# Seventeen projection jobs of a hybrid encoder block, from feature form to token form

## The reference

```
h = x + 0.5 * norm(swiglu(norm(x)))                    # FFN 1, inner width 5632
proj = norm(h) @ w_in                                  # pooling | z | x,B,C | dt | gates
A:  p -> trailing means over 2, 4, 8, 16 tokens (4 groups of 512 channels) minus p
      -> 512x512 map per group -> scale -> @ w_pool_out
B:  x,B,C -> causal depthwise conv over 4 tokens + SiLU; chunked state-space scan in 8 groups
      (8 heads of 64 each); * SiLU(z); norm; @ w_ssd_out
h = h + norm((sigmoid(gA) * A + sigmoid(gB) * B) @ w_mix_out)
k, v = norm(mem) @ w_k, w_v;  q = norm(h) @ w_q        # 4 heads of 128, 256 memory tokens
h = h + norm(attention(q, k, v) @ w_xo)
h = h + 0.5 * norm(swiglu(norm(h)))                    # FFN 2
```

## Time and profile before

| | us |
|---|---|
| median of three runs | 2731.94 |
| the profiled execution's own time | 2732.21 |
| its span in the trace | 2730.5 |
| TensorE matmul busy | 2717.9 |
| VectorE busy | 1631.0 |
| ScalarE busy | 1289.9 |
| GpSimd busy | 345.9 |

### The profile page before, as it was taken

The page is one execution under the profiler, slowest core; times in us unless marked ns, Lnnn a source line. Parts: engine busy times, 40 slices in busy tenths (PEclk is TensorE's granted clock), DMA queues, the critical chain, the costliest instruction groups (busy, mean ns, idle before and its releaser), DMA issues.

```text
span 2730.5 us, 39496 instructions
## 1 busy us (share of the span) xinstructions
PE 2717.9 (100%) x14076; PEld 2336.3 (86%) x14076; DVE 1631.0 (60%) x1920; ACT 1289.9 (47%) x1442; POOL 345.9 (13%) x619
## 2 busy tenths in 40 slices
PE   9999999999999999999999999999999999999998
PEld 7888888888899889989999888888988888888887
DVE  5555555544577556787887775566565555554444
ACT  5444444444454544455554564445654444444443
POOL 1121212000000000002122201223002122120000
PEclk9999999999999999999999999999999999999999
DMA  7777767666666665567667676668567677776664
GB/s 234 205 210 201 209 200 207 200 197 196 173 186 195 201 200 182 170 184 213 183 190 216 179 210 202 203 228 227 162 180 210 194 212 207 202 208 199 197 197 161
DMA packets 286770, 541.48 MB, mean 198 GB/s; under 512 B 27504, under 2 KB 28400, under 8 KB 286416
## 3 DMA queue, kind: packets, MB, share of 16 engines
q1 hardware_dynamic: 263520, 504.00, 60.7%
q0 software_dynamic: 22976, 36.07, 5.0%
q10 hardware_dynamic: 176, 0.07, 0.0%
HBM read 519.53 MB, written 2.16 MB: 191 GB/s over the span
## 4 chain that ended last, share of the span: by engine, by line
PE 98%; DVE 1%; DMA 0%; ACT 0%; issue 0%; DVEq 0%; ACTq 0%
PE J L660 26%; PE J L662 26%; PE J L661 26%; PE J L694 5%; PE J L697 5%; PE J L696 5%; PE J L737 1%; PE A L962 1%; PE A L963 1%; PE A L961 1%; PE J L733 0%; PE J L709 0%; DMA raw<-in_w_mix_out_dram 0%; PE J L674 0%; PE J L676 0%; PE J L675 0%
## 5 line engine op out<-in xcount | busy, mean ns | idle before, releaser
L1509 DVE TENSOR_TENSOR wl<-raw,wh 128x1024 fp32r<-128x1024 f32 x950 | 1154.5, 1222 | 961.8 <-ACT wh L1093 956.2
L1093 ACT ACTIVATE wh<-raw 128x1024 fp32r<-128x1024 f32 x950 | 1005.1, 1060 | 1305.2 <-PE J L662 1046.5
L660 PE MATMUL J<-wh,ul 128*128 128x512 f32 x2016 | 786.0, 390 | 2.3 <-DVE wl L1509 2.1
L662 PE MATMUL J<-wl,uh 128*128 128x512 f32 x2016 | 784.5, 389 | 0.0
L661 PE MATMUL J<-wh,uh 128*128 128x512 f32 x2016 | 784.4, 389 | 0.0
L660 PEld LDWEIGHTS J<-wh,ul 128*128 128x128 f32 x2016 | 378.6, 188 | 82.1 <-issue 4.0
L662 PEld LDWEIGHTS J<-wl,uh 128*128 128x128 f32 x2016 | 378.5, 188 | 79.0
L661 PEld LDWEIGHTS J<-wh,uh 128*128 128x128 f32 x2016 | 378.6, 188 | 77.5
L694 PE MATMUL J<-ul,wh 128*128 128x256 f32 x1056 | 300.2, 284 | 0.0
L697 PE MATMUL J<-uh,wl 128*128 128x256 f32 x1056 | 298.8, 283 | 0.0
L696 PE MATMUL J<-uh,wh 128*128 128x256 f32 x1056 | 298.8, 283 | 0.0
(11 more groups left out here) (293 smaller groups left out, 2262.4 us busy)
## 6 DMA issues: line engine op xcount, KB each, us to landing
raw<-in_ffn_w_dram SPq DMA_DIRECT2D x528, 512.0 KB, 4.3
raw<-in_w_in_dram SPq DMA_DIRECT2D x257, 512.0 KB, 3.9
raw<-in_w_ssd_out_dram SPq DMA_DIRECT2D x64, 512.0 KB, 3.6
raw<-in_w_pool_out_dram SPq DMA_DIRECT2D x32, 512.0 KB, 4.1
raw<-in_w_mix_out_dram SPq DMA_DIRECT2D x32, 512.0 KB, 6.2
hraw<-turned POOLq DMA_DIRECT2D x320, 32.0 KB, 4.0
csb<-cs_dram POOLq DMA_DIRECT2D x16, 512.0 KB, 7.4
raw<-in_pool_w_dram SPq DMA_DIRECT2D x8, 512.0 KB, 4.7
```

Of the source, the lines that this page charges most:

```text
L660: nc.tensor.matmul(o[:, t], b, wh[:, r, kk], start=(k == 0 and kk == 0), stop=False)
L662: mm = nc.tensor.matmul(o[:, t], a, wl[:, r, kk], start=False, stop=(k == last_k and kk == CK - 1))
L1093: nc.scalar.activation(wh[:, r], raw[:, r], ACT.Copy).then_inc(high, 1)
L1509: nc.vector.tensor_tensor(wl[:, r], raw[:, r], wh[:, r].bitcast(F32), ALU.subtract).then_inc(low, 1)
```

## The change

All 17 jobs are issued in token form. For each of them there are now four steps where there was one: ScalarE copies the PSUM tile to SBUF with the row norm as its scale (`tokens_out`, two instructions; for k one plain copy), VectorE turns it by 32x32 squares (`turn_tokens`, two transposes), GpSimd issues 16 DMAs of 32 KB that carry the blocks to where pooling and convolution read (`move_tokens`), and the reader waits for all of them (`f_moved`). One buffer `f_turn` serves all jobs but k, and one number `f_turned` counts them.

The places move too. Pooling's window starts 4 chunks after the end of the job behind (`end(pw)+4`) instead of at the end of its own; the taps of C0 start 5 chunks after C0, those of B1 in C1 after the masked squares (5 chunks), those of C1 in the first x job (5 chunks), those of x 5 chunks after x. The SiLU of x, its eight transposes on TensorE and its copy move to the next group: transposes after 2 chunks of x, the scan after 5 (3 before). The subtractions of the decay rows are split around the variance. GpSimd loads the next `csb` rows first, then moves x, then y of the group before.

```diff
+            def move_tokens(name, dst):
+                pool.wait_ge(f_turned, f_number(name) + 1)
+                move_natural(dst, f_turn, f_moved)
...
+            for g in range(GROUPS):
+                if g < GROUPS - 1:
+                    pool.wait_ge(seg_ready, g + 1)
+                    load_csb(g + 1)
+                move_tokens(("x", g), x_in)
+                if g >= 1:
+                    move_y(g - 1)
...
+            def tokens_out(name, dst, i=None, per=0):
+                n = f_number(name)
+                act.wait_ge(used, lin(end(name), i, per))
+                if n >= 1 or i is not None:
+                    act.wait_ge(f_turned, lin(n, i, 1))
+                for t in range(T):
+                    a = nc.scalar.activation(dst[:, t], tok(slot(name))[:, t], ACT.Copy, scale=sr_u[:, t:t + 1])
+                a.then_inc(evacuated[slot(name)], 1)
...
-            def conv_in(name, i=None, per=0):
-                done(i, per)
-                o = bc_in if i is None and isinstance(name, str) else x_in
-                nc.vector.tensor_tensor(o[:], feat(slot(name)), rbc[:].unsqueeze(1).to_broadcast([P, M, S]),
-                                        ALU.mult).then_inc(evacuated[slot(name)], 1)
+            def turn_tokens(name, src, i=None):
                 dve.wait_ge(evacuated[slot(name)], lin(moved(name), i, 1))
+                turn_blocks(f_turn, src, f_turned)
             def conv_taps(name, dst, blk, i=None, per=0, blk_per=0):
...
+                dve.wait_ge(f_moved, lin(256 * (f_number(name) + 1), i, 256))
...
+            for g in range(3):
+                to(end(f"pin{g + 1}"))
+                turn_tokens(f"pin{g + 1}", f_raw)
+                if g == 0:
+                    dve.wait_ge(t_ready[1], use(1, "csT"))
+                    nc.vector.tensor_copy(cst[:], A[:, 1, 0, 0:P]).then_inc(t_moved[1], 1)
+                pool_mixed(g)
+                to(end(f"pw{g}") + 4)
+                pool_window(g + 1)
+                to(end(f"pw{g}") + 6 + g // 2)
+                pool_low(g + 1)
...
+                to(c0 + CD, i, per)
+                turn_tokens(("x", 0), zs, i)
+                if i is not None:
+                    to(c0 + CD + 1, i, per)
+                    finish_scale(0, i - 1)
+                to(c0 + CD + 4, i, per)
...
                 weigh(slice(0, HPG // 2), 0, i)
+                to(c0 + CD + 5, i, per)
+                if i is None:
+                    cb_masked(1, 1)
+                conv_taps(("x", 0), xc, 0, i, per, M)
```

More of the change, by code:

```diff
@@ L386, in hybrid_block, with f_number @@
         CONVS = ["B0", "C0", "B1", "C1", ("x", 0)]
+        TURNED_JOBS = ["pin0", "pin1", "pin2", "pin3", "B0", "C0", "B1", "C1"] + [("x", g) for g in range(GROUPS)]
+        def f_number(name):
+            return TURNED_JOBS.index(name)
         def turned_before(f):
@@ L591, in _ @@
             pool.wait_ge(cs_stored, 16)
+            for g in range(1, 4):
+                move_tokens(f"pin{g}", pool_x)
             pool.wait_ge(pooled_low, len(WINDOWS))
@@ L878, in _ @@
             claim("pin0")
-            after_halves("pin0", 1, feature=True)
-            feature_chunks("pin0", uh, ul, range(4, 7), CD - 1, before=pre_wait(1))
+            after_halves("pin0", 1)
+            token_chunks("pin0", uh, ul, range(4, 7), CD - 1, before=pre_wait(1))
             pe.wait_ge(normed, 2)
@@ L964, in ssd, with turn_x @@
                 mm.then_inc(t_ready[1], 1)
+            def turn_x(i=None):
+                pe.wait_ge(xc_silu, GROUPS if i is None else i)
+                n = use(0, ("xT", 0)) - 1
+                pe.wait_ge(t_moved[0], n + GROUPS - 1 if i is None else lin(n - 1, i, 1))
+                for t in range(T):
+                    for m in range(M):
+                        tr = nc.tensor.transpose(A[:, 0, t, m * P:(m + 1) * P], xc[:, m, t * P:(t + 1) * P], ident[:])
+                tr.then_inc(t_ready[0], 1)
             def group(i=None):
@@ L1265, in _ @@
             pre_norm_behind(1)
+            def tokens_out(name, dst, i=None, per=0):
[3 more added lines that the diff above has]
+                    act.wait_ge(f_turned, lin(n, i, 1))
+                for t in range(T):
+                    a = nc.scalar.activation(dst[:, t], tok(slot(name))[:, t], ACT.Copy, scale=sr_u[:, t:t + 1])
+                a.then_inc(evacuated[slot(name)], 1)
+            to(end("pin0"))
+            act.wait_ge(normed, 2)
+            tokens_out("pin0", f_raw)
             to(end("dt") + 2)
@@ new lines, in group @@
+                if i is not None:
+                    to(c0 + 1, i, per)
+                    weigh(slice(HPG // 2, HPG), 0, i - 1).then_inc(w_ready, 1)
+                    to(c0 + 3, i, per)
+                    scale_x(0, i - 1)
+                    to(c0 + 6, i, per)
+                    finish_gate(0, i - 1)
+                    to(c0 + 7, i, per)
+                else:
+                    to(c0 + 2)
+                dve.wait_ge(csb_loaded, lin(16 * T, i, 16 * T))
+                subtract(range(HPG // 2))
@@ L1992, in group @@
+                if i is not None:
                     finish_var(0, i - 1)
+                else:
+                    to(c0 + 3)
+                subtract(range(HPG // 2, HPG)).then_inc(seg_ready, 1)
                 if i is None:
                     to(c0 + 5)
[L1995 to L2001 removed]
@@ L2002, in group @@
-                for h in range(HPG):
-                    def scalar(row):
-                        return small[:, row, h:h + 1] if i is None else small[:, row, bass.ds(i * HPG + h, 1)]
-                    nc.vector.tensor_scalar(E[:, h, 0:P], csb[:, h, 0], scalar(CS), 0.0, ALU.subtract, ALU.min)
-                    nc.vector.tensor_scalar(E[:, h, P:2 * P], csb[:, h, 1], scalar(REM), 0.0, ALU.add, ALU.min)
-                    l = nc.vector.tensor_scalar(E[:, h, 2 * P:3 * P], csb[:, h, 1], scalar(CS + 1), 0.0, ALU.subtract, ALU.min)
-                    if h == HPG // 2 - 1:
-                        to(c0 + 7, i, per)
```

262 lines of the change are left out of this document (134 added, 128 removed).

## The result

| | before | after | ratio |
|---|---|---|---|
| time, median | 2732.07 us | 2746.65 us (2745.12 to 2748.52, 5 runs) | 1.0053, 95% interval 1.0040 to 1.0066 |
| profiled execution | 2732.2, span 2730.5 | 2745.12, span 2743.5 | |

The changed kernel is 14.6 us slower, where I had forecast 10 us faster. In the profiled executions the loss is 13.0 us of span, and this is what has to be explained: my sum ended at 2722.2 for the profiled one, so it misses 22.9.

A forecast was written before the change was run, and what follows sets the result against it. TensorE's instruction spacings bound the kernel. Savings of 21.8 and 0.5 us against waits of 6.2, 0.35, 3.3, 0.85 and 1.6 gave -10.0, from 2732.2 to 2722 us; range 2711 to 2734.

The forecast's parts named there:

- token form, with the first group's stall: All 17 jobs: 0.16 us less a chunk over 136 chunks, -21.8 us, and -0.5 for TensorE's waits in first z.
- groups 1 to 7, stops: TensorE waits 0.9 us for late splits at the end of z in each of seven groups: +6.2 us.
- B1, C1, first x and z: Waits in the first jobs' chain of turns and taps: 0.35, 3.3 and 0.85 us.
- pooling: TensorE waits for pooll 1.35 us in group 3 and 0.25 in group 1: +1.6 us.
- Rival D: Token form saves less, 4.2 us by the page's formula, if something else sets the spacing: 2740 us; chance 0.05.
- I take 4.1, the middle: Landing after the last of sixteen issues, before work needing the data starts: 4.1 us, from rows of 3.42 to 4.89.
- T = E + 18.0: Groups 1 to 7: the taps of x start 18.0 us after x's end, where no wait needs 17.1.
- at 5.5, the bound that I gave: Upper end for the landing, the median of mem_raw's moves: time 2740 us.
- each us later costs about 12: Each us of later landing costs about 12 us, as there are 12 waits.
- Rival B: Moves about 2 us slower, from y's scalings and transposes beside the issues and csb's 1 MB: 2746 us; chance 0.12.
- Rival C, the lock: VectorE's reciprocal and y scalings hold GpSimd's issue at most 1.0 us in seven groups: 2729 us; chance 0.16.
- C1's 3.3 us: C1's taps stand in the first x job, so z's first split is late and TensorE waits 3.3 us.

The follow-up runs named there:

- e5: The changed kernel without the moves of the eight x jobs; the taps of x read f_turn directly: 2717.45 us, 0.9945 of before.
- e2: The changed kernel with csb's load for the next group issued behind x's and y's moves instead of ahead of them: 2738.22 us, 1.0020 of before.
- e10: The changed kernel with csb's load issued behind the copy of X, taps at their old place: 2737.22 us, 1.0018 of before.
- e9: The changed kernel with x's taps one chunk later, csb's load behind the copy of X, the sums' store behind pin1's moves: 2719.02 us, 0.9951 of before.
- e7: The changed kernel with x's taps one chunk later and csb's load behind the moves of x and y: 2729.73 us, 0.9999 of before.
- e3: The changed kernel with x's moves first, then a wait for their landing, then csb's load and y's moves: 2745.40 us, 1.0049 of before.
- e11: The kernel of e9 once more, with more rounds beside the kernel before on one chip: 2718.37 us, 0.9949 of before.

## Why the prediction was wrong, point by point

| step | forecast, us | measured, us |
|---|---|---|
| token form, with the first group's stall | -22.3 | about -20 |
| groups 1 to 7, stops | +6.2 | +20.0 |
| the lower clock behind them | no term | +7 to +9, of a rest of 9.8 |
| B1, C1, first x and z | +4.5 | about 0 |
| pooling | +1.6 | +2.9 |

The second and third row are the 29.8 us by which seven periods exceed those of e5: 20.0 are the stops and 9.8 remain, of which six drops of 1.1 to 1.5 us are 7 to 9. With 0.4 for the squares of B and C the sum is +13, as measured; but the first row is itself a rest, so this sum is no proof of it.

- **Token form: right.** -1.24 instead of -1.28 a job. In e5 the waits over those of before make 5 us and the time is 14.9 below before, so the form brings about 20; the last 2 us are spread in pieces that I did not trace. Rival D is out.
- **The step that failed: "I take 4.1, the middle" for the landing, and with it T = E + 18.0.** The mechanism was right: late splits behind late taps stop TensorE at the start of each x job. Turn, issue and the formula for the stop were right within 0.3 us. The size of this term was not: the landing was 5.6 to 6.4 us, and the seven stops are 20.0 us instead of 6.2. I had noted that no row shows this way "beside a csb load just issued", and took a middle of rows without such a load. e2 and e10 bring it to 4.5 to 4.9 in eleven groups of fourteen by taking csb away; in the other three, and in the changed kernel's last group, it is 5.6 to 6.2 without csb, and why stays open. A case named as unlike the rows should have been priced at their upper end: at 5.5, the bound that I gave, the sum was 2740.
- **The step that was missing: what a stop does behind itself.** No row of before has a stop in mid-kernel above 1 us, so the trace could not show it, but a sum of waits of 3 us had to leave room for it. My "each us later costs about 12" came out true by luck, in another way: 2 us later cost 24, by seven stops and six drops, not by twelve waits.
- **Rival B gave 2746 and the time is 2746.65.** The hit is luck too, as it is made of twelve waits. Of its two causes, csb's megabyte in the same queue is borne out (up to 1.4 of the 2 us). Its other one, y's scalings beside the issues, costs 0.2.
- **Rival C, the lock, is there, and small.** One of the sixteen issues runs beside y's two scalings (1421.81 to 1422.71, above):

```profile
1422.06 0.80 POOL L563 DMA_DIRECT2D x_in<-f_turn  x1
```

  It took 0.80 us and ended 0.15 behind them, where the other fifteen of this group took 0.585 to 0.594. The same issue is the long one in all seven groups that have scalings (0.79 to 0.80 us), and in the first group, which has none, no issue is long. So it costs 0.2 us a group, not 1.0. The rule of the Trainium skill, "SBUF — State Buffer", section "A bandwidth-pool intuition that's wrong (but worth ruling out)", has GpSimd wait for the end of a VectorE operation that holds the shared port; these rows agree with it.
- **C1's 3.3 us did not come**, since its landing was shorter than 4.1, not longer. GpSimd's issues in the changed kernel, VectorE's taps, and the window between them:

```profile
1130.87 9.35 POOL L563 DMA_DIRECT2D bc_in<-f_turn  x16 [15.53 <-DVE f_turn L1759]
```

```profile
1142.00 1.39 DVE L1869 TENSOR_SCALAR cT<-bc_in,cols 128x256 f32<-128x256 f32 x4 [1.07 <-DMA bc_in<-f_turn]
```

```profile
1140.20:1142.00 1.80, 1.80 (x10) 1.49 (x9) 0.73 (x1) 0.79 (x1) 1.78 (x3) 1.00 0.63 109
```

  The taps started 1.8 us after the last issue, and in that stretch the DMA engines were 63% busy, against 106% in e2's and 107% in the changed kernel's group. That is 2.3 of the 3.3 us; where the remaining 1.0 went I did not trace. In C0 and B1 the landing was 4.0 and 4.1, as I had taken it. In most other runs TensorE does stop at the first z, for 0.55 to 1.2 us. That this row came out at zero took 4.5 us off the miss.
- **Pooling.** Group 3 waited 1.6 where I had 1.35. Group 1 waited 1.3 where I had 0.25; e9, which moves the store of the sums behind pin1's moves, has no stop there. So the store was the cause, as I had it, but it held the moves for 3.3 us (from its issue at 794.25) instead of 2.35:

```profile
797.58 9.23 POOL L563 DMA_DIRECT2D pool_x<-f_turn  x16 [2.75 <-DMA cs_dram<-cst]
```

- The range, 2711 to 2734, ended where twelve waits of 1 us more would, and took in neither the upper bound of the landing nor a price behind the stops.

## What to carry to other kernels

When an edit replaces a path inside an engine by DMAs, price the landing by the transfers that will stand beside it, not by the median of similar moves: sixteen moves of the same size were in place 1.8 to 6.4 us after their last issue in the changed kernel. What else the DMA engines had to carry accounts for a part of this. Put the bulk load that nobody needs soon behind the work that everybody waits for, and look at whom it meets there; then give the consumer a chunk of slack in the static order. In this kernel a stop of some 3 us mostly cost a third to a half as much again by the clock behind it, so the first stops to remove are the long ones.

## What the runs showed of the hardware that I had not expected

- In the twelve profiled executions of the changed kernel and its variants, 27 stops in and around the groups were 2.3 to 4.2 us long, and behind 22 of them TensorE's granted clock was at its lower level for some 3.5 us (0.51 to 0.55 in the windows above). Of the shorter ones only e7's of 1.95 us had a drop, 0.50 for 9.9 us. Eleven matmuls that feed nothing, put into the wait, kept it at 1.00.
- Executions of a kernel with stops can differ by several us: e7 from 2723 to 2753, e10 from 2732 to 2740, where the kernel before stays within 2 us but for one execution at 2735.2. In e7 the mean granted clock goes with it (0.999 in the fastest, 0.991 in the slowest); in e10 executions at 0.999 lie from 2731.8 to 2739.9, so there the clock is not all of it.
- An issue of the same move took 0.59 us on GpSimd (9.42 for 16) and 0.66 on SyncE (5.25 for 8).
- In the first group GpSimd stopped for 5.4 to 6.3 us in the middle of its sixteen issues wherever csb's load no longer stood right ahead of them (e2, e3, e7, e9, e10, e11), with nothing that released it; in the changed kernel that pause is 0.85. The moves of B0 have a like pause in the changed kernel, of 6.26 us, where nobody waits for them. Its cause is open.
